# Spacing the groups of seven block products in a gated feed-forward loop: three plain units between groups instead of two

## The chip, the cores and the metric

The kernel runs on one core of a Trainium2 chip. The metric is the device time of one execution in microseconds (us). The engines that matter here are TensorE (PE in the profile; the loading of its stationary operand has a row of its own, PEld), VectorE (DVE), ScalarE (ACT) and SyncE (SP), which issues the transfers. Each engine runs its own instructions strictly in the order in which they are written; semaphores order them against one another.

## The reference

One block of a streaming encoder, for 256 tokens of width 2048:

```python
def swiglu(x, w_in, w_out):
    gate, up = jnp.split(x @ w_in, 2, axis=-1)
    return (jax.nn.silu(gate) * up) @ w_out

h = h + 0.5 * swiglu(rmsnorm(h, ffn1_norm[l]), ffn1_w_in[l], ffn1_w_out[l])
...   # gated mixing and stick-breaking attention, then cross attention
h = h + 0.5 * swiglu(rmsnorm(h, ffn2_norm[l]), ffn2_w_in[l], ffn2_w_out[l])
return rmsnorm(h, final_norm)
```

`w_in` is 2048 x 11264 (5632 gate columns, 5632 up columns). The change is in how `x @ w_in` is walked, in both feed-forward parts.

## The kernel before, in words

**Split products.** All data are 32-bit. Each operand is held as a high part (ACT copies the raw values, rounded, into `w_hi`) and a low part (DVE subtracts, `w_lo = raw - w_hi`), and each product is three matmuls: hi x hi, hi x lo, lo x hi. So every weight needs a transfer, one ACT instruction and one DVE instruction before TensorE may read it.

**Units and the ring.** A unit is 128 x 1024 weights (512 KB): two blocks of 128 rows by 512 columns. Units pass through a ring of four slots. SP may load unit p into its slot once the low part of unit p-4 is done (`load`, semaphore `w_lo_done`). ACT may write `w_hi` of unit p once TensorE is done with unit p-4 (`split`, semaphore `w_used`).

**A pair.** The hidden columns go in 11 chunks of 512. The first chunk is done plainly; the other ten are the loop `Fori(1, FJ)`, one gate chunk and one up chunk together, called a pair: 16 units, numbered 0 to 15. Ten pairs in each feed-forward part, 20 in all. A pair has three groups (`FAST = 3`, s = 0, 1, 2; called groups 1, 2 and 3 here) and ten plain units. A plain unit is 12 matmuls. A group takes two units, in which four weight blocks are laid out so that seven block products (21 matmuls) do the work of eight: it needs sums of weight blocks, which DVE makes (`weight_sums`, four additions of 128 x 512, into `raw` and `t_raw`), ACT rounds (`t_hi_part`) and DVE subtracts (`t_lo_part`). The first two of the seven products need only the units themselves; the other five wait for `t_lo_part`. The products of the groups go partly into banks of their own: `sum_p1` and `sum_p5` (tile `tp`), `sum_p6` and `sum_p7` (tile `aux`).

**The order of a pair on DVE.** For each group: the four sums (`L1314` to `L1323`), which first wait for both units of the group to have landed; `w_lo` of its two units (`L1190`); `t_lo_part` (`L1335`); then `w_lo` of the plain units after it. After group 1's first plain unit stands `up_drained` (`L1290`), and among group 2's sums stand the two halves of `hidden` (`L1297`), both for the pair before. After group 3 and `w_lo` of unit 12 come, in this order: the transpose of the hidden chunk of the pair before, fetched by SP (`turn`, `L1230`); `sum_p6` plus a copy of `sum_p1` (`L1352`), which waits for ACT's copy (`p1_copied`); the low part of the hidden chunk (`fill_lo`, `L1198`), which waits for ACT's high part (`L735`); `w_lo` of unit 13; three additions that finish the gate (`L1356`, `L1361`, `L1363`); `w_lo` of unit 14; one subtraction (`L1368`); `w_lo` of unit 15. Then the next pair begins.

**ACT** runs beside it: `w_hi` of the units (`L728`), `t_hi_part` (`L825`), and between the `w_hi` of units 12 and 13 a wait for TensorE to be done with group 3 (`w_used` up to `FAST_END`), the copy of `sum_p1` (`L837`) and the high part of the hidden chunk (`L735`); after unit 14 the silu (`L844`), and then unit 15.

**SP** issues the 16 loads of a pair in order, and between them `send` (the hidden chunk to a buffer in device memory, 512 KB, once `hid_done` says that it is there) and `fetch` (four transfers that bring it back in turned order, once `send` has landed).

Of the kernel before, what the change touches and what calls it, by code (L numbers as in the profile page):

```python
# [29 lines left out]


FAST = 3


def pair_order():

    plain = [(0, u) for u in range(FAST, U8)] + [(1, u) for u in range(FAST, U8)]
    order = []
    for s in range(FAST):
        order += [("fast", s), ("fast", s)] + plain[:2]  # L40
        plain = plain[2:]
    return order + plain


# [2 lines left out]

FAST_END = FAST_AT[-1] + 2

GATE_END = PAIR_ORDER.index((0, U8 - 1)) + 1  # L50
UP_START = PAIR_ORDER.index((1, FAST))

SEND_AT = 10
FETCH_AT = 12

X_MIX_AT = [5, 7, 9]
H3_MIX_AT = [9, 11, 13]
# [132 lines left out]
def encoder_block(nc, x, x_cols, mem, mem_cols, first_cols, ws_cols, ffn1_w_in, ffn1_w_out, w_mix_in,  # L190
# [8 lines left out]
    with ctx:  # L199
# [511 lines left out]
        def _(eng):  # L711
# [8 lines left out]
            def split(base, n, u, length=U8, after_long=False, wait=True):  # L720

                loads = slot_loads(base, u % RING) + u // RING + rate(u, length) * n

                eng.wait_ge(w_loaded[u % RING], 16 * loads + 16)
                if wait:

                    eng.wait_ge(w_used, base + length * n + (u - ring_distance(u, after_long) + 1))
                eng.activation(w_hi[:, u % RING], raw[:, u % RING], ACT.Copy).then_inc(w_hi_done, 1)  # L728
# [72 lines left out]
            def ffn_in(base, rs, first, hid, first_hi):  # L801

                def silu(gate_used):

                    eng.wait_ge(stat_out, stat(rs) + 1)

                    eng.wait_ge(w_used, gate_used)

                    eng.wait_ge(mix_lo_done, FAST * (fast_pairs[base] > 0) + FAST)
                    for t in range(NT):  # L810
                        last = eng.activation(stage[:, t], acc[:, t], ACT.Silu,
                                              scale=rstd[:, stat(rs), t:t + 1])
                    last.then_inc(silu_done, 1)

                def fast_hi(j, s):


                    p = FAST_AT[s]
                    eng.wait_ge(t1_done, fast_count(base, j, s) + 1)
                    split(base, j, p, PAIR)  # L820
                    split(base, j, p + 1, PAIR)
                    eng.wait_ge(t_summed, fast_count(base, j, s) + 1)
                    if s:
                        eng.wait_ge(t_used, fast_count(base, j, s))
                    eng.activation(t_hi_part[:], t_raw[:], ACT.Copy).then_inc(t_hi_done, 1)  # L825

                def pair(j, hid_dst):

                    for s in range(FAST):
                        fast_hi(j, s)  # L830
                        split(base, j, FAST_AT[s] + 2, PAIR)
                        split(base, j, FAST_AT[s] + 3, PAIR)
                    for p in range(4 * FAST, PAIR - 3):
                        split(base, j, p, PAIR)

                    eng.wait_ge(w_used, base + PAIR * j + FAST_END)
                    eng.activation(copy_p1, sum_p1, ACT.Copy).then_inc(p1_copied, 1)  # L837
                    fill_hi(turned, number(TURNS, hid) + j, hid_dst, src=stage4)
                    split(base, j, PAIR - 3, PAIR)
                    split(base, j, PAIR - 2, PAIR)  # L840

                    eng.wait_ge(gate_added, fast_pairs[base] + j)
                    for t in range(NT):
                        last = eng.activation(stage[:, t], stage[:, t], ACT.Silu,  # L844
                                              scale=rstd[:, stat(rs), t:t + 1])
                    last.then_inc(silu_done, 1)
                    split(base, j, PAIR - 1, PAIR)

                first(silu)
                with eng.Fori(1, DC + 1) as j:  # L850
                    pair(j, first_hi[:, bass.ds(4 * j - 4, 4), :])
                with eng.Fori(DC + 1, FJ) as j:
                    pair(j, hid_hi[:, bass.ds(4 * j - 4 - KT, 4), :])
# [323 lines left out]
        def _(eng):  # L1177
# [106 lines left out]
            def ffn_in(base, rs, first, hid, first_hi, first_lo):  # L1284
                def up_drained(j):


                    eng.wait_ge(gate_read, silus[base] + 1 + j)
                    eng.wait_ge(w_used, base + PAIR + PAIR * j)
                    eng.tensor_tensor(shared[:], acc[:, NT:2 * NT], shared[:], ALU.subtract).then_inc(up_read, 1)  # L1290
# [34 lines left out]
                def unit_lo(j, p):  # L1325

                    split(p, base + PAIR * j + p)
# [10 lines left out]
                def pair(j, hi, lo):  # L1338
                    done = fast_pairs[base] + j

                    for s in range(FAST):
                        fast_lo(j, s)
                        unit_lo(j, FAST_AT[s] + 2)
                        if s == 0:
                            up_drained(j - 1)
                        unit_lo(j, FAST_AT[s] + 3)
                    for p in range(4 * FAST, PAIR - 3):
                        unit_lo(j, p)
                    turn(number(TURNS, hid) - 1 + j, stage4)

                    eng.wait_ge(p1_copied, done)
                    eng.tensor_tensor(shared[:, 0], sum_p6, copy_p1, ALU.add).then_inc(p6_added, 1)  # L1352
                    fill_lo(split_number(hid) - 1 + j, lo, hi, src=stage4)
                    unit_lo(j, PAIR - 3)
                    eng.wait_ge(p6_added, done)
                    eng.tensor_tensor(shared[:, 1], shared[:, 0], sum_p7, ALU.subtract).then_inc(p7_added, 1)  # L1356

                    eng.wait_ge(w_used, base + PAIR * j + GATE_END)

                    eng.wait_ge(t_read, number(FILLS, hid) + j)  # L1360
                    eng.tensor_tensor(stage[:, 0], acc[:, 0], copy_p1, ALU.add)  # L1361
                    eng.wait_ge(p7_added, done)
                    eng.tensor_tensor(stage[:, 1], acc[:, 1], shared[:, 1], ALU.add).then_inc(gate_added, 1)  # L1363
                    unit_lo(j, PAIR - 2)

                    eng.wait_ge(gate_added, done)
                    p5 = sum_p5.rearrange("p (a n) -> p a n", a=1).broadcast_to([P, NT, CH])
                    eng.tensor_tensor(shared[:], shared[:], p5, ALU.subtract).then_inc(gate_read, 1)  # L1368
                    unit_lo(j, PAIR - 1)
# [495 lines left out]
        def _(eng):  # L1865
# [29 lines left out]
            def ffn_in(base, hi, lo, first):  # L1895
# [6 lines left out]
                def block_of(k, t):  # L1902
                    rows = slice(t * P, (t + 1) * P)
                    return hi[:, k, rows], lo[:, k, rows]
# [7 lines left out]
                def fast(j, s):  # L1912


                    p = FAST_AT[s]
                    unit = base + PAIR * j + p
                    start, stop = s == 0, s == FAST - 1
                    s3, s1, s2 = [(mix_hi[s][:, i], mix_lo[s][:, i]) for i in range(3)]
                    eng.wait_ge(w_lo_done, unit + 1)
                    three(sum_p1, block_of(UK * s, 0), ring_block(p, 1), start, stop)  # L1920
                    three(sum_p5, s1, ring_block(p, 0), start, stop).then_inc(w_used, 1)

                    eng.wait_ge(t_lo_done, fast_count(base, j, s) + 1)
                    three(sum_p7, s3, sum_block(0), start, stop)
                    three(sum_p6, s2, sum_block(1), start, stop)
                    three(acc[:, 1], block_of(UK * s + 1, 1), sum_block(2), start, False).then_inc(t_used, 1)

                    eng.wait_ge(w_lo_done, unit + 2)
                    three(acc[:, 0], block_of(UK * s + 1, 0), ring_block(p + 1, 0), start, False)
                    if s == 0:  # L1930
                        eng.wait_ge(up_read, silus[base] + j)
                    three(acc[:, NT], block_of(UK * s, 1), ring_block(p + 1, 1), start, False).then_inc(w_used, 1)

                def plain(j, p):

                    side, u = PAIR_ORDER[p]
                    eng.wait_ge(w_lo_done, base + PAIR * j + p + 1)
                    for i in range(UK):
                        for t in range(NT):
                            start = p == UP_START and i == 0 and t == 1  # L1940
                            stop = u == U8 - 1 and i == UK - 1
                            last = three(acc[:, NT * side + t], block_of(UK * u + i, t), ring_block(p, i), start, stop)
                    last.then_inc(w_used, 1)

# [417 lines left out]
```

## Time and profile before

| | |
|---|---|
| median of 3 runs | 2129.9 us (2128.22 to 2129.93) |
| the profiled execution | 2127.3 us, its span 2125.4 us |
| TensorE busy | 2107.7 us, 99% of the span |
| VectorE busy | 1530.6 us (72%); in the pair loops 355.1 us of 381.7 |
| ScalarE busy | 1093.8 us (51%) |
| DMA | 472.37 MB, 222 GB/s on average |
| granted TensorE clock | 1.00 in each of the stretches read |

The page's busy shares are for the whole span. The first part's pair loop lies from 49 to about 474 us, the second's from 1454 to about 1878 us; what is between and behind them has no groups and isn't touched. "Start to start" below means the distance between the start times of two rows of the trace, which is the pace at which an engine takes its instructions; the durations printed overlap a little at both ends.

### The profile page before, as it was taken

The page shows a single profiled execution, that of the slowest core. Times are in us where ns is not written, and L with a number is a line of the kernel's source. Part 1 is how long each engine was busy: PE and PEld are TensorE (multiplying, and loading weights), DVE is VectorE, ACT ScalarE, POOL GpSimd, SP SyncE. Part 2 cuts the span into 40 slices and gives each one's busy share as a digit, 9 for nine tenths or more (in the row PEclk, how much of TensorE's full clock was granted, in tenths as well). Part 3 has the DMA queues.
Part 4 walks back from the last instruction along what each step waited for, and adds up shares of the span by engine and source line. Part 5 has one row for each costly group of instructions (what it writes and reads, how often), then busy time and mean ns, then how long its engine had stood idle before and what let it go on. Part 6 is the DMA issues. An engine that isn't in the chain of part 4 may idle for free.

```text
span 2125.4 us, 27293 instructions
## 1 busy us (share of the span) xinstructions
PE 2107.7 (99%) x9405; PEld 1738.6 (82%) x9405; DVE 1530.6 (72%) x1647; ACT 1093.8 (51%) x1251; POOL 38.3 (2%) x50
## 2 busy tenths in 40 slices
PE   9999999999999999999999999999999999999998
PEld 7778888878888888888888888887888887888887
DVE  8989999984555576566565656569999999964444
ACT  7555555553444465456544545555555555543433
POOL 0000000000000030000000000000000000000000
PEclk9999999999999999999999999999999999999999
DMA  8676667676566676765487766576667666785554
GB/s 297 212 236 224 218 221 234 222 257 228 203 234 210 227 258 217 241 215 185 175 286 239 235 208 195 187 243 209 219 214 236 226 217 211 238 286 195 191 187 157
DMA packets 185317, 472.37 MB, mean 222 GB/s; under 512 B 17056, under 2 KB 67616, under 8 KB 185120
## 3 DMA queue, kind: packets, MB, share of 16 engines
q1 hardware_dynamic: 183088, 464.11, 65.3%
q0 software_dynamic: 1728, 6.82, 0.9%
q8 instruction: 42, 0.69, 0.1%
q10 hardware_dynamic: 432, 0.53, 0.1%
q14 instruction: 27, 0.22, 0.0%
HBM read 443.60 MB, written 27.79 MB: 222 GB/s over the span
## 4 chain that ended last, share of the span: by engine, by line
PE 60%; DVE 18%; issue 9%; DMA 9%; ACT 3%; DVEq 0%; ACTq 0%; SPq 0%; POOL 0%; POOLq 0%
PE acc L1875 18%; PE acc L1878 18%; PE acc L1877 18%; DMA raw<-in_ffn_w_in 9%; DVE w_lo L1190 8%; DVE t_raw L1319 2%; DVE raw L1315 2%; DVE t_raw L1314 2%; ACT w_hi L728 1%; DVE stage L1230 1%; PE acc L2035 1%; DVE t_raw L1323 1%; DVE stage L1297 1%; PE acc L1899 1%; PE acc L1898 1%
## 5 line engine op out<-in xcount | busy, mean ns | idle before, releaser
L1190 DVE TENSOR_TENSOR w_lo<-raw,w_hi 128x1024 fp32r<-128x1024 f32 x765 | 924.1, 1223 | 476.1 <-ACT w_hi L728 473.5
L728 ACT ACTIVATE w_hi<-raw 128x1024 fp32r<-128x1024 f32 x765 | 794.4, 1055 | 839.0 <-PE acc L1878 530.6
L1875 PE MATMUL acc<-w_hi,a_hi 128*128 128x512 f32 x744 | 290.0, 390 | 0.0
L1877 PE MATMUL acc<-w_lo,a_hi 128*128 128x512 f32 x744 | 289.6, 389 | 0.0
L1878 PE MATMUL acc<-w_hi,a_lo 128*128 128x512 f32 x744 | 289.5, 389 | 0.0
L1875 PE MATMUL acc<-w_hi,b_hi 128*128 128x512 f32 x576 | 225.6, 392 | 0.0
L1878 PE MATMUL acc<-w_hi,b_lo 128*128 128x512 f32 x576 | 224.2, 389 | 0.0
L1877 PE MATMUL acc<-w_lo,b_hi 128*128 128x512 f32 x576 | 224.2, 389 | 0.0
L1898 PE MATMUL acc<-w_hi,b_hi 128*128 128x512 f32 x460 | 179.0, 389 | 0.0
L1898 PE MATMUL acc<-w_hi,a_hi 128*128 128x512 f32 x460 | 179.0, 389 | 0.0
L1899 PE MATMUL acc<-w_lo,b_hi 128*128 128x512 f32 x460 | 178.9, 389 | 0.0
L1900 PE MATMUL acc<-w_hi,a_lo 128*128 128x512 f32 x460 | 178.9, 389 | 0.0
L1899 PE MATMUL acc<-w_lo,a_hi 128*128 128x512 f32 x460 | 178.9, 389 | 0.0
L1900 PE MATMUL acc<-w_hi,b_lo 128*128 128x512 f32 x460 | 178.9, 389 | 0.0
L1875 PE MATMUL acc<-w_hi,hid_hi 128*128 128x512 f32 x432 | 168.0, 389 | 0.0
L1877 PE MATMUL acc<-w_lo,hid_hi 128*128 128x512 f32 x432 | 168.0, 389 | 0.0
L1878 PE MATMUL acc<-w_hi,hid_lo 128*128 128x512 f32 x432 | 168.0, 389 | 0.0
L1875 PEld LDWEIGHTS acc<-w_hi,a_hi 128*128 128x128 f32 x744 | 139.7, 188 | 29.6 <-issue 0.9
L1878 PEld LDWEIGHTS acc<-w_hi,a_lo 128*128 128x128 f32 x744 | 139.7, 188 | 29.1
L1877 PEld LDWEIGHTS acc<-w_lo,a_hi 128*128 128x128 f32 x744 | 139.7, 188 | 28.7
L1878 PEld LDWEIGHTS acc<-w_hi,b_lo 128*128 128x128 f32 x576 | 108.1, 188 | 22.7
L1875 PEld LDWEIGHTS acc<-w_hi,b_hi 128*128 128x128 f32 x576 | 108.2, 188 | 22.4 <-issue 0.8
(276 smaller groups left out, 2645.0 us busy)
## 6 DMA issues: line engine op xcount, KB each, us to landing
raw<-in_ffn_w_in SPq DMA_DIRECT2D x349, 512.0 KB, 4.3
raw<-in_ffn_w_out SPq DMA_DIRECT2D x176, 512.0 KB, 4.3
raw<-in_w_mix_in SPq DMA_DIRECT2D x80, 512.0 KB, 4.4
raw<-in_w_ckv SPq DMA_DIRECT2D x64, 512.0 KB, 4.3
memq<-bounce SPq DMA_DIRECT2D x196, 128.0 KB, 3.4
bounce<-stage SPq DMA_DIRECT2D x37, 512.0 KB, 6.1
raw<-in_w_mix_out SPq DMA_DIRECT2D x32, 512.0 KB, 4.4
raw<-in_w_cq SPq DMA_DIRECT2D x32, 512.0 KB, 4.3
```

Source lines behind the costliest of these rows:

```text
L728: eng.activation(w_hi[:, u % RING], raw[:, u % RING], ACT.Copy).then_inc(w_hi_done, 1)
L1190: eng.tensor_tensor(w_lo[:, u % RING], raw[:, u % RING], w_hi[:, u % RING].bitcast(f32), ALU.subtract).then_inc(w_lo_done, 1)
L1230: eng.transpose(dst.rearrange("p k (b j) -> p b k j", j=32), xs.rearrange("p b (k i) -> p b k i", i=32)).then_inc(turned, 1)
L1314: eng.tensor_tensor(t_raw[:, 0], b12, b22, ALU.add)
L1315: eng.tensor_tensor(b12, b12, b11, ALU.add).then_inc(t1_done, 1)
L1319: eng.tensor_tensor(t_raw[:, 1], b12, b22, ALU.add).then_inc(t2_done, 1)
L1875: eng.matmul(dst, x_hi[:, rows], w_hi[:, slot, i], start=start and i == 0, stop=False)
L1877: eng.matmul(dst, x_hi[:, rows], w_lo[:, slot, i], start=False, stop=False)
L1878: last = eng.matmul(dst, x_lo[:, rows], w_hi[:, slot, i], start=False, stop=stop and i == UK - 1)
L1898: eng.matmul(dst, x[0], w[0], start=start, stop=False)
L1899: eng.matmul(dst, x[0], w[1], start=False, stop=False)
L1900: return eng.matmul(dst, x[1], w[0], start=False, stop=stop)
```

## The change

The order of a pair gets three plain units after group 1 and three after group 2 (`BETWEEN = 3`), where it had two, and so four after group 3 instead of six. The groups now take units 0 and 1, 5 and 6, 10 and 11 (before: 0 and 1, 4 and 5, 8 and 9). The ten plain units keep their order among themselves. `send` moves from ahead of load 10 to ahead of load 9, `fetch` from ahead of load 12 to ahead of load 13. The wait of the gate additions on TensorE (`GATE_END`) now names the end of group 3, since the gate's last plain unit comes before it. `FAST_END`, which ACT's copy of `sum_p1` waits for, is unit 12 instead of 10 in number: the end of group 3 in both. What each engine does after `w_lo` of unit 12 keeps its order.

```diff
+BETWEEN = 3
...
     for s in range(FAST):
-        order += [("fast", s), ("fast", s)] + plain[:2]
-        plain = plain[2:]
+        order += [("fast", s), ("fast", s)] + plain[:BETWEEN]
+        plain = plain[BETWEEN:]
     return order + plain
...
-GATE_END = PAIR_ORDER.index((0, U8 - 1)) + 1
+GATE_END = FAST_END
...
-SEND_AT = 10
-FETCH_AT = 12
+SEND_AT = 9
+FETCH_AT = 13
...  (ACT)
                     for s in range(FAST):
                         fast_hi(j, s)
-                        split(base, j, FAST_AT[s] + 2, PAIR)
-                        split(base, j, FAST_AT[s] + 3, PAIR)
-                    for p in range(4 * FAST, PAIR - 3):
-                        split(base, j, p, PAIR)
+                        for p in range(FAST_AT[s] + 2, (FAST_AT + [PAIR - 3])[s + 1]):
+                            split(base, j, p, PAIR)
...  (DVE)
                     for s in range(FAST):
                         fast_lo(j, s)
-                        unit_lo(j, FAST_AT[s] + 2)
-                        if s == 0:
-                            up_drained(j - 1)
-                        unit_lo(j, FAST_AT[s] + 3)
-                    for p in range(4 * FAST, PAIR - 3):
-                        unit_lo(j, p)
+                        for p in range(FAST_AT[s] + 2, (FAST_AT + [PAIR - 3])[s + 1]):
+                            unit_lo(j, p)
+                            if p == FAST_AT[0] + 2:
+                                up_drained(j - 1)
...  (PE, flags that end an accumulation)
-                    three(acc[:, 1], block_of(UK * s + 1, 1), sum_block(2), start, False).then_inc(t_used, 1)
+                    three(acc[:, 1], block_of(UK * s + 1, 1), sum_block(2), start, stop).then_inc(t_used, 1)
...
-                    three(acc[:, 0], block_of(UK * s + 1, 0), ring_block(p + 1, 0), start, False)
+                    three(acc[:, 0], block_of(UK * s + 1, 0), ring_block(p + 1, 0), start, stop)
...
-                            stop = u == U8 - 1 and i == UK - 1
+                            stop = side == 1 and u == U8 - 1 and i == UK - 1
```

**DVE, from group 3's `t_lo_part` to the hidden chunk's low part, in the first pair loop.** Before, three `w_lo` (units 10, 11, 12) stand between `t_lo_part` and the transpose:

```order
L1335 TENSOR_TENSOR t_lo_part<-t_raw,t_hi_part 128x1536
L1189 REGISTER_ALU
L1190 TENSOR_TENSOR w_lo<-raw,w_hi 128x1024
L1189 REGISTER_ALU
L1190 TENSOR_TENSOR w_lo<-raw,w_hi 128x1024
L1189 REGISTER_ALU
L1190 TENSOR_TENSOR w_lo<-raw,w_hi 128x1024
L1229 ISA
L1230 STREAM_TRANSPOSE stage<-memq 128x8x4x32
L1352 TENSOR_TENSOR shared<-aux,arrived 128x512
```

The same place in the changed kernel (its line numbers are one to three lower) has one, unit 12:

```order
L1334 TENSOR_TENSOR t_lo_part<-t_raw,t_hi_part 128x1536
L1188 REGISTER_ALU
L1189 TENSOR_TENSOR w_lo<-raw,w_hi 128x1024
L1228 ISA
L1229 STREAM_TRANSPOSE stage<-memq 128x8x4x32
L1349 TENSOR_TENSOR shared<-aux,arrived 128x512
```

Two `w_lo` have gone from this stretch, and nothing behind it has moved.

**DVE, from group 2's `t_lo_part` to group 3's sums, same loop.** Before there are two `w_lo` between (units 6 and 7):

```order
L1335 TENSOR_TENSOR t_lo_part<-t_raw,t_hi_part 128x1536
L1189 REGISTER_ALU
L1190 TENSOR_TENSOR w_lo<-raw,w_hi 128x1024
L1189 REGISTER_ALU
L1190 TENSOR_TENSOR w_lo<-raw,w_hi 128x1024
L1310 ISA
L1314 TENSOR_TENSOR t_raw<-raw 128x512
```

Now there are three (units 7, 8 and 9):

```order
L1334 TENSOR_TENSOR t_lo_part<-t_raw,t_hi_part 128x1536
L1188 REGISTER_ALU
L1189 TENSOR_TENSOR w_lo<-raw,w_hi 128x1024
L1188 REGISTER_ALU
L1189 TENSOR_TENSOR w_lo<-raw,w_hi 128x1024
L1188 REGISTER_ALU
L1189 TENSOR_TENSOR w_lo<-raw,w_hi 128x1024
L1309 ISA
L1313 TENSOR_TENSOR t_raw<-raw 128x512
```

The third stands ahead of the sums in the queue; the stretch after group 1 gets a third `w_lo` in the same way.

**SP, around `send`, same loop.** Before (the rows from load 8 on; `bounce<-stage` is `send`):

```order
L450 DMA raw<-in_ffn_w_in 128x1024
L450 ISA [waits w_lo_done]
L450 DMA raw<-in_ffn_w_in 128x1024
L457 ISA [waits hid_done]
L457 DMA bounce<-stage 128x2x512
L450 ISA [waits w_lo_done]
L450 DMA raw<-in_ffn_w_in 128x1024
```

After:

```order
L451 DMA raw<-in_ffn_w_in 128x1024
L458 ISA [waits hid_done]
L458 DMA bounce<-stage 128x2x512
L451 ISA [waits w_lo_done]
L451 DMA raw<-in_ffn_w_in 128x1024
L451 ISA [waits w_lo_done]
L451 DMA raw<-in_ffn_w_in 128x1024
```

`send` and its wait have moved ahead of load 9.

## Rows read from the trace of the kernel before

**Rows 1.** The page, section 1: busy time of each engine over the whole span
```profile
PE 2107.7 (99%) x9405; PEld 1738.6 (82%) x9405; DVE 1530.6 (72%) x1647; ACT 1093.8 (51%) x1251; POOL 38.3 (2%) x50
```

**Rows 2.** Who waited for whom, whole span: us in total, times, longest us
```profile
DVE t_raw L1314 <- issue: 37.2, 20, 2.9
...
ACT arrived L837 <- PE acc L1900: 29.6, 20, 1.9
...
PEld aux L1898 <- DVE t_lo_part L1335: 24.2, 40, 1.6
```

**Rows 3.** Stretches of nine pairs: us, PE, PEld, DVE, ACT, POOL busy, clock, DMA share, GB/s
```profile
49.44:431.18 381.74, 377.83 (x1648) 307.75 (x1647) 355.11 (x371) 208.57 (x209) 0.00 (x0) 1.00 0.68 223
1454.43:1836.47 382.04, 377.57 (x1649) 307.70 (x1647) 353.41 (x370) 207.78 (x207) 0.00 (x0) 1.00 0.68 222
```

**Rows 4.** TensorE in order of time, group 3 of pair 5 to pair 6
```profile
243.12 0.50 PE L1898 MATMUL aux<-t_hi_part,mix_hi 128*128 128x512 f32 x1 [0.26 <-DVE t_lo_part L1335]
...
246.42 0.39 PE L1900 MATMUL acc<-w_hi,a_lo 128*128 128x512 f32 x1
246.65 0.39 PE L1898 MATMUL acc<-w_hi,a_hi 128*128 128x512 f32 x1
...
262.97 0.39 PE L1898 MATMUL tp<-w_hi,a_hi 128*128 128x512 f32 x1
```

**Rows 5.** DVE in order of time, same stretch: start, us, what, [idle before]
```profile
236.38 0.69 DVE L1314 TENSOR_TENSOR t_raw<-raw 128x512 f32<-128x512 f32 x1 [1.80 <-issue]
...
242.98 3.49 DVE L1190 TENSOR_TENSOR w_lo<-raw,w_hi 128x1024 fp32r<-128x1024 f32 x3
246.39 1.23 DVE L1230 STREAM_TRANSPOSE stage<-memq 128x1024 f32<-128x1024 f32 x1
247.55 0.65 DVE L1352 TENSOR_TENSOR shared<-aux,arrived 128x512 f32<-128x512 f32 x1
248.99 1.23 DVE L1198 TENSOR_TENSOR hid_lo<-stage,hid_hi 128x1024 f32 x1 [0.79 <-ACT hid_hi L735]
250.14 1.22 DVE L1190 TENSOR_TENSOR w_lo<-raw,w_hi 128x1024 fp32r<-128x1024 f32 x1
...
253.07 1.22 DVE L1190 TENSOR_TENSOR w_lo<-raw,w_hi 128x1024 fp32r<-128x1024 f32 x1
...
255.51 1.23 DVE L1190 TENSOR_TENSOR w_lo<-raw,w_hi 128x1024 fp32r<-128x1024 f32 x1
256.65 0.68 DVE L1314 TENSOR_TENSOR t_raw<-raw 128x512 f32<-128x512 f32 x1
...
259.31 2.35 DVE L1190 TENSOR_TENSOR w_lo<-raw,w_hi 128x1024 fp32r<-128x1024 f32 x2
261.58 1.75 DVE L1335 TENSOR_TENSOR t_lo_part<-t_raw,t_hi_part 128x1536 fp32r<-128x1536 f32 x1
263.25 1.22 DVE L1190 TENSOR_TENSOR w_lo<-raw,w_hi 128x1024 fp32r<-128x1024 f32 x1
264.38 1.22 DVE L1290 TENSOR_TENSOR shared<-acc,shared 128x1024 f32<-128x1024 f32 x1
...
266.65 0.68 DVE L1314 TENSOR_TENSOR t_raw<-raw 128x512 f32<-128x512 f32 x1
...
270.38 2.35 DVE L1190 TENSOR_TENSOR w_lo<-raw,w_hi 128x1024 fp32r<-128x1024 f32 x2
```

**Rows 6.** ACT in order of time, same stretch
```profile
246.85 0.60 ACT L837 ACTIVATE arrived<-tp 128x512 f32<-128x512 f32 x1 [1.65 <-PE acc L1900]
247.76 1.06 ACT L735 ACTIVATE hid_hi<-stage 128x1024 f32 x1 [0.32 <-DVE stage L1230]
```

**Rows 7.** The chain that ended last, around pairs 5 and 6: start, us, what
```profile
230.81 3.77 DMA raw<-in_ffn_w_in
...
261.83 4.29 DMA raw<-in_ffn_w_in
```

**Rows 8.** SP's issues in order of time
```profile
231.34 0.41 SPq L457 DMA_DIRECT2D bounce<-stage  x1
```

## The prediction

> **What bounds the kernel now.** I read the page first: TensorE is busy for 2107.7 of 2125.4 us [rows 1], so at first sight nothing but its own pace counts. The waits show where the missing time is: the load of the first operand after `t_lo_part` waited 24.2 us in 40 of the 60 groups, DVE stood idle before a group's sums 37.2 us in 20 cases (one per pair, always group 3), and ACT waited 29.6 us, 20 times, for TensorE's end of group 3 before it copied `sum_p1` [rows 2]. Then I took the pair loops alone: nine pairs last 381.74 us in the first part and 382.04 in the second, so a pair takes 42.43 us. DVE is busy 39.4 us of each (355.11 and 353.41 over nine), at a granted clock of 1.00 [rows 3]. TensorE's own pace: from 246.65 to 262.97 it starts 72 matmuls (six plain units), 0.2267 us each [rows 4]. 183 matmuls make 41.5 us. So a pair loses only about 0.9 us to stalls, 17 us over 20 pairs, and that is the whole prize if every stall in the groups went.
>
> DVE is thus 3 us per pair from being the bound itself, and where its work stands matters more than how much there is. The reader should follow one pair on DVE and ask, for each group, when `t_lo_part` is done and when TensorE wants it. TensorE wants it six matmuls (1.36 us) after the group starts. Before group 1 of pair 6 DVE was done at 263.25 [rows 5], TensorE wanted it at 262.97 + 1.36 = 264.33 [rows 4]: a slack of 1.1 us after a stretch in which TensorE had 93 matmuls (21.1 us) to do.
>
> **The change part by part.** No instruction is added or removed on TensorE, ACT or DVE: the same 183 matmuls and the same 39.4 us of DVE work per pair, and the flags that end an accumulation change no duration, 0 us. What changes is how much work of each engine lies between the three deadlines. TensorE's stretches become 57, 57 and 69 matmuls (12.92, 12.92 and 15.64 us) instead of 45, 45 and 93 (10.20, 10.20, 21.08). I time everything from A, the start of the first matmul on `t_lo_part` in a group (243.12 for group 3 [rows 4]).
>
> *Group 3 to the next group 1.* Before, DVE did three `w_lo`, the transpose and then `sum_p6`, which needs ACT's copy. The last matmul of group 3 starts at 246.42 [rows 4], the copy at 246.85, which is A + 3.73, and it takes 0.60 [rows 6]: ready at A + 4.33. DVE began the `sum_p6` step at 247.55 = A + 4.43 [rows 5], just as its earlier work ran out. Now two `w_lo` of 1.13 us each (start to start, 263.25 to 264.38 [rows 5]) are gone from ahead of it. DVE has finished the transpose by A + 2.2, but the copy still comes at A + 4.33, because it hangs on TensorE's 15 matmuls and not on DVE. So the 2.27 us that DVE no longer does here turn into idle time, and the `sum_p6` step stays at A + 4.43. What does get earlier is ACT's high part of the hidden chunk: it started at 247.76 only because the transpose was late [rows 6], and would now follow the copy directly at A + 4.33. The low part starts 1.23 after it (247.76 to 248.99 [rows 5, 6]), at A + 5.56 instead of A + 5.87. From there to the end of the next group 1's `t_lo_part` (248.99 to 263.25 [rows 5]) lie 14.26 us of DVE work with hardly a gap: fill, units 13, 14, 15, the gate's additions, four sums, two `w_lo`, `t_lo_part`. Ready at A + 19.82, and with the 0.14 from there to the matmul (242.98 to 243.12 [rows 4, 5]) the next A is at **A + 19.96**. Before it was A + 21.21 (262.97 + 1.36 - 243.12), set by TensorE. TensorE now has only 15.64 + 0.14 us of work there: it stalls for 4.2 us, spread over units 13 and 14, the first products of group 1 and the five behind them, the longest about 1.6 us (unit 13's `w_lo` is ready at A + 7.84, and unit 12 ends at A + 6.3).
>
> *Group 1 to group 2.* DVE's order is unit 2, `up_drained`, unit 3, unit 4, the sums with `hidden`, two `w_lo`, `t_lo_part`. Its work is 3.40 (263.25 to 266.65) + 1.13 + 3.73 (266.65 to 270.38) + 2.27 (259.31 to 261.58) + 1.67 (261.58 to 263.25) = 12.20 us [rows 5]. Its sums wait for load 6, which may be issued once unit 2's `w_lo` is done, 1.13 in. Load 5 took 4.29 us there [rows 7]; with 0.1 to issue and 0.2 to start, the sums begin at 5.7 instead of 4.5. That gives 5.75 + 3.73 + 2.27 + 1.67 = **13.42**, against TensorE's 12.92 (13.06 with the 0.14 of a restart). If the load lands in 3.77, as the other one in those rows did, TensorE's 13.06 stands.
>
> *Group 2 to group 3.* Three `w_lo`, sums, two `w_lo`, `t_lo_part`: 3.40 + 6.60 (236.38 to 242.98 [rows 5]) = 10.0 us. The sums wait for load 11, issued after unit 7's `w_lo`: 1.13 + 0.1 + 4.3 + 0.2 + 6.60 = 12.3, below TensorE's **12.92**, which I take. The other bound: before, from the end of unit 5's `w_lo` at 230.65 (228.37 + 2.28) to the sums at 236.38 went 5.7 us, idle 1.80 at the end [rows 5, 7], while `send` was issued at 231.34 [rows 8], right behind load 9. If load 11 suffers as much, 1.13 + 5.7 + 6.60 = 13.4. I take the lower, because `send` now goes out during group 2's sums, some 5 us ahead of load 11. `send` needs only `hidden`, which is done by then, so load 9 behind it waits for nothing new, and `fetch` has until A + 1 of group 3, over 10 us: 0 us for both.
>
> The Trainium skill ("DMA: Bandwidth & Descriptors", Anatomy of one DMA) puts a transfer at about 2.0 us fixed plus its bytes over 436 GB/s. By that a 512 KB load would take 3.2 us, an estimate from that page, and group 1 to 2 would be 13.06 instead of 13.42: 6 us less in the sum. The trace's loads of 3.77 and 4.29 us [rows 7] don't agree, so the sum goes by them.
>
> *The sum.* A pair: 19.96 + 13.42 + 12.92 = 46.30 us, against 42.43: +3.87. Nine such distances in each part: 18 x 3.87 = 69.7. The tenth pair has no group 1 behind it. There the end is unit 15, whose `w_lo` starts at A + 12.08 (255.51 - 243.12 less the 0.31 gained [rows 5]), ends 1.14 later, and is followed by 0.14 and 12 matmuls: A + 16.08. With the other two stretches 42.4 us, against 177 x 0.2267 + 0.9 = 41.0 before: +1.4, twice 2.8. Together +72.5 us. The profiled execution's 2127.3 becomes 2199.8; the median of the runs shown lies 2.6 above it, so I say **2202 us**.
>
> **The rivals.**
>
> *The groups' stalls go, as the wider spacing between them would have it* (faster). Between groups 1 and 2, and 2 and 3, DVE gains 2.72 us of TensorE's time for 1.13 of work, so the waits of rows 2 would vanish there. If group 1 then weren't late either, a pair takes 41.5 us: 17 us less, about 2113. It decides at a DVE stretch after group 3 below 15.8 us. Against it: the work behind the copy alone is 14.26 + 1.23, on top of the 4.33 to the copy's end. 5%.
>
> *No measurable change*, if ACT and DVE found some 4 us of that stretch to fill elsewhere. Their orders are written out and strict: 4%. (Below 0.2%, 4 us, a measurement of this kernel can't be told from none.)
>
> *DVE's idle time is used* (slower, but less). If the copy weren't what `sum_p6` waits for, the stretch would be 263.25 - 242.98 = 20.27 less two `w_lo`, 18.0, and the pair 18.0 + 0.14 + 13.42 + 12.92 = 44.5: +37, about 2167. For it: DVE at 247.55 started when its own work ended, too, so those rows don't say alone which of the two it needed. Against it: the copy's end at 247.45. 9%.
>
> *Loads are late as well* (slower still): 5.7 us for both loads 6 and 11. Then 14.8 + 13.4 + 19.96 = 48.2: +104 with the tenth pairs, about 2234. 6%.
>
> *TensorE's clock falls.* It stalled for up to 1.6 us at a time before [rows 2] at a clock of 1.00 [rows 3]; now there are four stalls in one stretch. If a third of a pair's matmuls, 61, ran at the lower level (1.2 instead of 2.4 GHz), that is 61 x 0.2267 = 13.8 us more where DVE didn't hide it, and even half of it over 20 pairs gives +138 on top, about 2340. No single stall that I find is longer than those of before. 3%. The rule behind it, that TensorE drops to the lower clock after a stretch of idling, is the Trainium skill's ("TensorE: Matmul & The Clock Gate", What's actually happening); the trace, with its clock of 1.00 throughout, has no case of it.
>
> **How the numbers follow.** My forecast, slower by the copy and the serial work behind it, has 73%; its own range is 2188 (group 1 to 2 at 13.06, and 0.4 less after group 3 where ACT's steps overlap) to 2222 (one load at 5.7). The range leaves out the first two cases and the last three for the most part: **2182 to 2224**. Faster 5%, same 4%, slower 91%.
>
> **What would show it.** Right: a period of about 46 us; ACT's high part of the hidden chunk starting right at the copy's end; DVE idle some 2 us before the `sum_p6` step (`shared<-aux,arrived`), 20 times; TensorE waiting for `w_lo` in the last units and for `t_lo_part` in group 1, where it waited for nothing; DVE's idle time before group 3's sums nearly without effect. Wrong: TensorE still waiting mainly in groups 2 and 3, a stretch from group 3's A to group 1's well under 19 us, or a granted clock below 1.

## The result and the profile after

The changed kernel takes 2195.6 us (median of 4 runs, 2195.05 to 2197.13) against 2129.06 us before in the same comparison. The ratio is 1.0315, with a 95% interval of 1.0299 to 1.033: slower by 66.5 us. The profiled execution has a span of 2193.3 us, against 2125.4, 67.9 more.

The page's first section of the changed kernel answers to [rows 1]. TensorE's busy share went from 99% to 97%, although the span is 3.2% longer; DVE and ACT have the same work in a longer span:

```profile
PE 2123.6 (97%) x9405; PEld 1734.8 (79%) x9405; DVE 1534.3 (70%) x1647; ACT 1090.8 (50%) x1251; POOL 38.3 (2%) x50
```

Busy time between the starts of the first and the tenth pair, in both parts of the changed kernel, columns as in [rows 3]. The clock is 1.00, nine pairs last 411.91 and 413.53 us instead of 381.74 and 382.04, and the work of DVE in them is what it was (354.55 and 352.96, before 355.11 and 353.41):

```profile
49.67:461.58 411.91, 384.43 (x1648) 305.83 (x1647) 354.55 (x369) 205.55 (x207) 0.00 (x0) 1.00 0.65 206
1487.17:1900.70 413.53, 385.22 (x1649) 305.55 (x1647) 352.96 (x369) 204.73 (x206) 0.00 (x0) 1.00 0.65 204
```

The waits of the changed kernel (us in total, times, longest), beside [rows 2]. Its line numbers are one to three lower than before: L836 is the copy of `sum_p1`, L1349 the `sum_p6` step, L1189 `w_lo`, L1334 `t_lo_part`, L1313 the first of the sums:

```profile
ACT arrived L836 <- PE acc L1897: 101.5, 20, 5.7
DVE t_raw L1313 <- DMA raw<-in_ffn_w_in: 54.7, 28, 2.8
DVE shared L1349 <- ACT arrived L836: 50.4, 20, 3.2
...
PEld acc L1895 <- DVE w_lo L1189: 43.7, 40, 1.9
PEld aux L1895 <- DVE t_lo_part L1334: 37.5, 35, 1.6
...
PE acc L1895 <- DVE w_lo L1189: 29.0, 20, 1.5
PE aux L1895 <- DVE t_lo_part L1334: 22.9, 25, 1.2
```

Two waits are new. DVE waits for ACT's copy in every pair, 2.5 us each, and TensorE waits for `w_lo` in the last plain units. Neither had a row before.

One pair shows how they hang together. First TensorE in order of time, from group 3 to the next group 1 (A is 261.16 and then 280.87). It reaches group 3's `t_lo_part` products without a stall, then stalls three times, before unit 13, before the first products of group 1 and before the five behind them:

```profile
261.16 0.39 PE L1895 MATMUL aux<-t_hi_part,mix_hi 128*128 128x512 f32 x1
...
264.34 0.39 PE L1897 MATMUL acc<-w_hi,a_lo 128*128 128x512 f32 x1
...
268.89 0.50 PE L1895 MATMUL acc<-w_hi,a_hi 128*128 128x512 f32 x1 [1.45 <-DVE w_lo L1189]
...
278.06 0.50 PE L1895 MATMUL tp<-w_hi,a_hi 128*128 128x512 f32 x1 [0.51 <-DVE w_lo L1189]
...
280.87 0.50 PE L1895 MATMUL aux<-t_hi_part,mix_hi 128*128 128x512 f32 x1 [1.15 <-DVE t_lo_part L1334]
281.21 0.39 PE L1896 MATMUL aux<-t_lo_part,mix_hi 128*128 128x512 f32 x1
```

Then ACT in the same stretch: 5.20 us of waiting for group 3's last matmul, the copy, and at once the high part of the hidden chunk:

```profile
264.76 0.60 ACT L836 ACTIVATE arrived<-tp 128x512 f32<-128x512 f32 x1 [5.20 <-PE acc L1897]
265.25 1.05 ACT L736 ACTIVATE hid_hi<-stage 128x1024 f32 x1
```

And DVE: the transpose is over early, 2.59 us of idle time follow, and behind the copy the work runs on almost without a gap until `t_lo_part` of the next group 1 is done at 280.73:

```profile
253.82 0.69 DVE L1313 TENSOR_TENSOR t_raw<-raw 128x512 f32<-128x512 f32 x1 [2.22 <-DMA raw<-in_ffn_w_in]
...
260.42 1.22 DVE L1189 TENSOR_TENSOR w_lo<-raw,w_hi 128x1024 fp32r<-128x1024 f32 x1
261.56 1.24 DVE L1229 STREAM_TRANSPOSE stage<-memq 128x1024 f32<-128x1024 f32 x1
265.39 0.69 DVE L1349 TENSOR_TENSOR shared<-aux,arrived 128x512 f32<-128x512 f32 x1 [2.59 <-ACT arrived L836]
266.48 1.23 DVE L1197 TENSOR_TENSOR hid_lo<-stage,hid_hi 128x1024 f32 x1 [0.40 <-ACT hid_hi L736]
...
280.73 1.22 DVE L1189 TENSOR_TENSOR w_lo<-raw,w_hi 128x1024 fp32r<-128x1024 f32 x1
```

The first of these rows shows the other thing to see: DVE also waited 2.22 us for load 11 before group 3's sums, and it cost nothing, since TensorE came to group 3 later still.

**Three distances.** To compare kernels, I took from each timeline of TensorE the start A of the first matmul on `t_lo_part` in every group, and averaged the distances over the pairs of each part. The first number is the first feed-forward part, the second the other; "floor" is TensorE's own matmuls at 0.2267 us. This table is used for the experiments too.

| kernel | group 1 to 2 | 2 to 3 | 3 to the next 1 | a pair |
|---|---|---|---|---|
| before | 10.50, 10.35 | 10.75, 10.85 | 21.20, 21.23 | 42.35, 42.45 |
| its floor | 10.20 | 10.20 | 21.08 | 41.5 |
| changed | 13.17, 13.38 | 13.01, 13.05 | 19.71, 19.72 | 45.90, 46.11 |
| its floor | 12.92 | 12.92 | 15.64 | 41.5 |
| e2_spacing_alone | 13.41, 13.32 | 13.27, 13.62 | 19.79, 19.83 | 46.56, 46.70 |
| e3_chunk_first | 13.41, 13.42 | 13.05, 13.05 | 17.23, 17.19 | 43.73, 43.61 |
| e4_three_two | 13.50, 13.37 | 10.34, 10.31 | 19.70, 19.71 | 43.59, 43.37 |
| e5_four_two | 15.99, 15.94 | 10.39, 10.36 | 19.77, 19.75 | 46.15, 46.02 |
| e1_moved_transfers | 10.54, 10.33 | 10.85, 10.88 | 21.24, 21.23 | 42.63, 42.47 |
| e6_unit13_first | 10.33, 10.21 | 10.71, 10.46 | 21.24, 21.19 | 42.30, 41.78 |
| e8_send8 | 10.92, 10.82 | 10.34, 10.33 | 21.46, 21.32 | 42.70, 42.44 |
| e7_both | 10.40, 10.29 | 10.31, 10.32 | 21.08, 21.09 | 41.82, 41.72 |
| e10_send8_fetch13 | 10.29, 10.21 | 10.21, 10.23 | 21.08, 21.08 | 41.59, 41.53 |
| e9_both_fetch13 | 11.02, 10.71 | 10.35, 10.33 | 21.22, 21.16 | 42.57, 42.20 |

Measured from A to A, nine pairs are 31.9 and 32.9 us longer in the changed kernel, 64.9 together. (The stretches above gave 30.2 and 31.5: they end where the tenth pair starts, before the stalls of its group 1.) The remaining 3.0 of the 67.9 lie behind the A of the tenth pairs' group 1 and at the ends.

The text also gives, for single loads, the time from issue to landing, as the median over the pairs of one part. Load 9 is the load of unit 9 of a pair, and so on.

### The profile page after: what moved, and what is told of

The parts are those of the page before. It is cut to its first block, busy times and chain, and to the rows that moved or that the text cites. A ratio compares the mean times of both kernels' runs of the same rounds, so it can differ in the third digit from the quotient of the medians.

```text
span 2193.3 us, 27333 instructions
## 1 busy us (share of the span) xinstructions
PE 2123.6 (97%) x9405; PEld 1734.8 (79%) x9405; DVE 1534.3 (70%) x1647; ACT 1090.8 (50%) x1251; POOL 38.3 (2%) x50
## 4 chain that ended last, share of the span: by engine, by line
PE 77%; DVE 10%; issue 6%; DMA 3%; ACT 3%; DVEq 0%; ACTq 0%; SPq 0%; POOLq 0%; POOL 0%
PE acc L1872 18%; PE acc L1875 18%; PE acc L1874 18%; PE acc L1895 5%; PE acc L1897 5%; PE acc L1896 5%; DVE w_lo L1189 4%; DMA raw<-in_ffn_w_in 2%; DVE t_lo_part L1334 2%; PE aux L1895 1%; PE aux L1896 1%; PE aux L1897 1%; ACT w_hi L729 1%; DVE t_raw L1318 1%; DVE raw L1314 1%
## 5 line engine op out<-in xcount | busy, mean ns | idle before, releaser
L1189 DVE TENSOR_TENSOR w_lo<-raw,w_hi 128x1024 fp32r<-128x1024 f32 x765 | 923.8, 1224 | 464.9 <-ACT w_hi L729 462.4
L1895 PE MATMUL acc<-w_hi,a_hi 128*128 128x512 f32 x460 | 181.4, 394 | 14.5 <-DVE w_lo L1189 14.5
L1895 PE MATMUL acc<-w_hi,b_hi 128*128 128x512 f32 x460 | 181.4, 394 | 14.5 <-DVE w_lo L1189 14.5
```

What stands on the lines that cost most here:

```text
L1189: eng.tensor_tensor(w_lo[:, u % RING], raw[:, u % RING], w_hi[:, u % RING].bitcast(f32), ALU.subtract).then_inc(w_lo_done, 1)
L1895: eng.matmul(dst, x[0], w[0], start=start, stop=False)
```

## The experiments

Theory A, from the prediction: the loss is the serial work of ACT and DVE that starts when TensorE ends group 3, which four plain units no longer cover. The rivals on test: B, the moved transfers; C, DVE's whole work as the bound; D, the units between the groups and the loads that their sums wait for.

**The transfers moved alone, and the spacing alone.** First the kernel before with only the two constants of the change:

```diff
-SEND_AT = 10
-FETCH_AT = 12
+SEND_AT = 9
+FETCH_AT = 13
```

> The spacing of before (two and two), with send ahead of load 9 and fetch ahead of load 13. Theory A (the loss is the serial work that begins with ACT's copy at the end of group 3, which four plain units no longer cover): within 6 us of before, since the order of the units is that of before; a few us less if send then disturbs load 9 less. Rival B (the moved transfers make the group sums late): a good part of the 66 us, 2150 or more.

Measured: 2133.06 us against 2127.27, ratio 1.0027 (1.0017 to 1.0037). The 5.8 us are just within theory A's 6, with the sign that I had thought the less likely. Then the changed kernel with the constants put back to 10 and 12:

> The changed spacing, with send and fetch where before had them (ahead of loads 10 and 12). Theory A: 2190 to 2205, as the changed kernel or a few us above, since send then goes out just ahead of loads 10 and 11, on which group 3's sums wait. Rival B: back near 2130.

Measured: 2206.31 us, ratio 1.0367 (1.0344 to 1.039), 10.7 us above the changed kernel. So the spacing makes the whole loss, and in the changed kernel the moved transfers give some of it back. The table shows where: with `send` (issued at 250.02 in this timeline) just ahead of loads 10 and 11, group 2 to 3 goes from 13.01 and 13.05 to 13.27 and 13.62. The waits of this kernel say the same, 49 stalls on `t_lo_part` instead of 35:

```profile
PEld aux L1895 <- DVE t_lo_part L1334: 51.6, 49, 1.6
```

Rival B is out.

**The work that needs no copy put first.** The changed kernel, with this on ACT:

```diff
+                    split(base, j, PAIR - 3, PAIR)
+                    fill_hi(turned, number(TURNS, hid) + j, hid_dst, src=stage4)
                     eng.wait_ge(w_used, base + PAIR * j + FAST_END)
                     eng.activation(copy_p1, sum_p1, ACT.Copy).then_inc(p1_copied, 1)
-                    fill_hi(turned, number(TURNS, hid) + j, hid_dst, src=stage4)
-                    split(base, j, PAIR - 3, PAIR)
```

and on DVE:

```diff
+                    unit_lo(j, PAIR - 3)
+                    fill_lo(split_number(hid) - 1 + j, lo, hi, src=stage4)
                     eng.wait_ge(p1_copied, done)
                     eng.tensor_tensor(shared[:, 0], sum_p6, copy_p1, ALU.add).then_inc(p6_added, 1)
-                    fill_lo(split_number(hid) - 1 + j, lo, hi, src=stage4)
-                    unit_lo(j, PAIR - 3)
```

> The changed kernel, with the work that needs no copy of sum_p1 put ahead of the wait for it: on ACT the high parts of unit 13 and of the hidden chunk, on DVE w_lo of unit 13 and the low part of the chunk. Same instructions, other order. Theory A: the 2.6 us of idle time before the sum_p6 step and the 0.4 behind it are filled, the stretch from group 3 to group 1 falls from 19.7 to about 17.5 us, the pair from 45.9 to 43.7, the time by about 40 us to 2155. Rival C (a pair is long because DVE's whole work has become the bound, wherever its idle time stands): the idle time comes back elsewhere, 2190 or more.

Measured: 2150.87 us, ratio 1.0109 (1.0084 to 1.0134), 44.7 us less than the changed kernel. Group 3 to group 1 fell from 19.7 to 17.2 us; of the other distances only group 1 to 2 of the first part moved, up by 0.24. DVE in order of time shows the gap closed, `w_lo` of unit 13 and the chunk's low part standing where it idled:

```profile
254.85 1.24 DVE L1229 STREAM_TRANSPOSE stage<-memq 128x1024 f32<-128x1024 f32 x1
256.01 1.18 DVE L1189 TENSOR_TENSOR w_lo<-raw,w_hi 128x1024 fp32r<-128x1024 f32 x1
257.45 1.23 DVE L1197 TENSOR_TENSOR hid_lo<-stage,hid_hi 128x1024 f32 x1 [0.27 <-ACT hid_hi L736]
258.60 0.68 DVE L1351 TENSOR_TENSOR shared<-aux,arrived 128x512 f32<-128x512 f32 x1
```

The same instructions in another order give back two thirds of the loss, which rival C does not allow. The 17.2 us that are left are DVE's own work between the two groups: 20.27 before, less two `w_lo` (2.27) and the idle 0.79, is 17.2. TensorE has 15.6 of its own there.

**The same number of units behind group 3, otherwise spread.** The spacing as a list, `BETWEEN = [4, 2, 0]`, leaves four behind group 3 as the change does:

```diff
-BETWEEN = 3
+BETWEEN = [4, 2, 0]
...
-        order += [("fast", s), ("fast", s)] + plain[:BETWEEN]
-        plain = plain[BETWEEN:]
+        order += [("fast", s), ("fast", s)] + plain[:BETWEEN[s]]
+        plain = plain[BETWEEN[s]:]
```

> Four plain units after group 1, two after group 2, four after group 3 (the changed kernel: 3, 3, 4). Theory A: only the number behind group 3 counts, so the pair is 15.6 + 10.8 + 19.7 = 46.1 us and the time 2190 to 2205. Rival D (three units between groups are what costs, through the sums that wait for loads after each): another time than the changed kernel's by more than 15 us, since one of the stretches is now longer and one shorter.

Measured: 2198.46 us, ratio 1.0336 (1.0312 to 1.036), within 3 us of the changed kernel, and the distance behind group 3 is 19.75 again. With `[3, 2, 0]`, five behind group 3:

> Three plain units after group 1, two after group 2, five after group 3. Theory A: the stretch from group 3 to group 1 stays at the 19.7 us of its serial work, although TensorE now has 18.4 + 0.1 us of its own there; 13.2 + 10.8 + 19.7 = 43.7 us a pair, 1.3 above before, 2150 to 2157. Rival D (units between the groups cost, one by one): half of the 66 us, 2162.

Measured: 2145.76 us, ratio 1.0092 (1.0077 to 1.0108), below the range that I gave: group 2 to 3 took 10.3 and not 10.8, and group 1 to 2 13.4 to 13.5 and not 13.2. The waits on the copy, in this kernel and then in the other one, go with it (DVE waits about 0.7 us longer per pair with one unit fewer):

```profile
DVE shared L1349 <- ACT arrived L836: 31.0, 20, 1.9
```

```profile
DVE shared L1349 <- ACT arrived L836: 45.4, 20, 2.8
```

The distance from group 3 to group 1 is thus 19.7 us with four units behind group 3 and with five, whose floors are 15.6 and 18.4 us, and nearly TensorE's 21.1 with six. That is a constant length of serial work that six units cover and five don't.

Rival D, a cost per unit between the groups, is out by this run and the table. Five units between the groups instead of six should have left half of the 66 us, 2162. And the distances 1 to 2 and 2 to 3 lie only 0.1 to 0.7 us above TensorE's floor, with two, three or four units in between, the kernel before included. The run with four and two alone could not have told it: it has six units between the groups, as the change has.

**Toward a faster kernel.** In the kernel before, DVE idled twice in a pair: 1.80 us before group 3's sums, and 0.79 before the chunk's low part [rows 5]. First the second one. On DVE the low part and unit 13 change places, on ACT the `w_hi` of unit 13 goes ahead of the wait for group 3:

```diff
+                    split(base, j, PAIR - 3, PAIR)
                     eng.wait_ge(w_used, base + PAIR * j + FAST_END)
                     eng.activation(copy_p1, sum_p1, ACT.Copy).then_inc(p1_copied, 1)
                     fill_hi(turned, number(TURNS, hid) + j, hid_dst, src=stage4)
-                    split(base, j, PAIR - 3, PAIR)
...
                     eng.tensor_tensor(shared[:, 0], sum_p6, copy_p1, ALU.add).then_inc(p6_added, 1)
-                    fill_lo(split_number(hid) - 1 + j, lo, hi, src=stage4)
                     unit_lo(j, PAIR - 3)
+                    fill_lo(split_number(hid) - 1 + j, lo, hi, src=stage4)
```

> The kernel before with one change of order: w_lo of unit 13 ahead of the low part of the hidden chunk on DVE, its w_hi ahead of ACT's wait for group 3. It takes away the 0.79 us in which DVE waits for ACT behind the sum_p6 step. If DVE's chain of work sets the pace of the pairs before too, 0.4 to 0.8 us a pair: 2112 to 2120. If TensorE's own work and the loads of group 3 set it, no change, within 4 us of before.

Measured: 2122.39 us against 2126.52, ratio 0.9981 (0.9972 to 0.999). A gain of 4 us, short of the 2112 to 2120 of the one theory and at the edge of the other's 4 us. The idle time is gone from where it was and partly back before the `sum_p6` step, where the kernel before had no row:

```profile
DVE shared L1352 <- ACT arrived L838: 10.8, 15, 0.8
```

Then the first one, `send` ahead of load 8:

```diff
-SEND_AT = 10
+SEND_AT = 8
```

> The kernel before with send ahead of load 8 instead of load 10, so that it no longer runs right behind load 9, on which group 3's sums wait. If send is what delays load 9, DVE's idle time there (37 us in 20 pairs) falls by a third or more and the time by 5 to 12 us. If the load itself is what takes so long, within 4 us of before, or a little above as with send ahead of load 9.

Measured: 2132.65 us, ratio 1.0026 (1.0012 to 1.004): slower, although the wait that it was meant for did fall from 37.2 us to this:

```profile
DVE t_raw L1314 <- issue: 14.8, 20, 1.0
```

Load 9 now landed 4.4 us after its issue instead of 5.4, and group 2 to 3 is 0.4 to 0.5 us shorter. DVE in order of time shows where the gain is lost. `w_lo` of unit 12 waits for its `w_hi`, and in ACT's timeline that waited for load 12, which goes out behind `fetch` and landed 5.1 us after its issue instead of 3.8 (first part):

```profile
244.01 1.23 DVE L1190 TENSOR_TENSOR w_lo<-raw,w_hi 128x1024 fp32r<-128x1024 f32 x1 [0.81 <-ACT w_hi L728]
```

```profile
242.91 1.06 ACT L728 ACTIVATE w_hi<-raw 128x1024 fp32r<-128x1024 f32 x1 [1.43 <-DMA raw<-in_ffn_w_in]
```

DVE has no slack from here to group 2 of the next pair, so the 0.8 us come out there: from group 3 by way of group 1 to group 2 it takes 32.38 and 32.14 us, 0.68 and 0.56 more than before.

Both edits together:

> Both of the changes above in one: unit 13 first, and send ahead of load 8. If the gains are of one chain they add, down to where TensorE's 41.5 us a pair is the floor: at most 17 us under before, 2110 to 2118; else the better of the two alone.

Measured: 2115.44 us, ratio 0.9949 (0.9936 to 0.9963). That is 11 us below before, where the edits alone gave 4 less and 6 more. The range that I gave is met, but neither of its reasons: the two together are worth more than their sum and more than the better alone. The table fits the wait on load 12 being absorbed by the 0.79 us that the first edit frees: from group 3 to group 2 it takes 31.48 and 31.38 us, below the 31.70 and 31.58 of before. The next kernel moves `fetch` out of load 12's way, with `send` ahead of load 8 and the order of ACT and DVE as before:

```diff
-SEND_AT = 10
-FETCH_AT = 12
+SEND_AT = 8
+FETCH_AT = 13
```

> The kernel before with send ahead of load 8 and fetch ahead of load 13. With send alone moved, DVE's idle time before group 3's sums fell from 37 to 15 us, but a new wait of 0.8 us a pair stood before w_lo of unit 12, whose load goes out behind fetch, and the time rose. If load 12 behind fetch is what took the gain, it is gone here and the time is 2116 to 2124; if send running beside the loads of groups 2 and 3 costs by itself, it stays at 2127 or above.

Measured: 2111.98 us against 2127.37, ratio 0.9923 (0.991 to 0.9937), the fastest of all and better than expected. Load 12 lands 3.8 us after its issue again. A pair takes 41.59 and 41.53 us, TensorE's floor of 41.5. This kernel differs from the first experiment, the transfers moved alone, only in that `send` is ahead of load 8 and not of load 9, and takes 21 us less. Its page, and its busy time in nine pairs of the second part, in which TensorE has no idle time left:

```profile
PE 2099.2 (99%) x9405; PEld 1740.4 (82%) x9405; DVE 1534.6 (73%) x1647; ACT 1096.9 (52%) x1251; POOL 38.1 (2%) x50
```

```profile
1448.13:1821.88 373.75, 373.75 (x1649) 308.89 (x1647) 356.05 (x371) 209.19 (x207) 0.00 (x0) 1.00 0.70 228
```

Last, all three edits:

> Unit 13 first, send ahead of load 8 (together 2115 us) and fetch ahead of load 13. The pair was at 41.8 us, TensorE's own work is 41.5, so what is left to gain is 5 us: 2110 to 2116.

Measured: 2128.25 us, ratio 1.0007 (0.9998 to 1.0016). A clear miss. ACT in order of time shows why: with unit 13's `w_hi` ahead of the copy, the copy now also waits for load 13, and `fetch` stands ahead of exactly that load. DVE's row behind it is the idle time of the changed kernel once more:

```profile
248.89 1.06 ACT L728 ACTIVATE w_hi<-raw 128x1024 fp32r<-128x1024 f32 x1 [3.36 <-DMA raw<-in_ffn_w_in]
249.85 0.58 ACT L838 ACTIVATE arrived<-tp 128x512 f32<-128x512 f32 x1
```

```profile
250.47 0.69 DVE L1352 TENSOR_TENSOR shared<-aux,arrived 128x512 f32<-128x512 f32 x1 [2.48 <-ACT arrived L838]
```

## Why the prediction was right

It said 2202 us, 2182 to 2224; measured were 2195.6. Against the profiled executions the sum was +72.5 for a span that grew by 67.9; the rest of the difference is the 2.6 us that were added for the distance from the profiled execution to the median, which was 0.2 in the changed kernel. Term by term:

- *Group 3 to group 1:* said 19.96, measured 19.71 and 19.72. The mechanism is as predicted: the copy hangs on TensorE's 15 matmuls and not on DVE, so DVE's two `w_lo` less became 2.59 us of idle time, and ACT's high part followed the copy at once. In the pair shown TensorE stalled in three of the four places named; unit 14 had no stall. The 0.25 too much has two sources in the rows. Group 3 no longer started with a stall, so the copy came 3.60 after A (261.16 to 264.76) and not 3.73; and ACT starts its next instruction 0.49 behind the start of the copy, where I had counted its full 0.60.
- *Group 1 to 2:* said 13.42, measured 13.17 and 13.38. Load 6 landed 3.91 us after its issue in the first part and 4.31 in the second, where I took 4.29. In one pair of the first part unit 2's `w_lo` ended at 236.19 and the sums began at 240.15, 3.96 later instead of 4.6.
- *Group 2 to 3:* said 12.92, TensorE's floor, measured 13.01 and 13.05. Load 11 landed after 4.35 and 4.60 us, where I took 4.3. DVE's idle time there (2.22 in the pair shown) cost almost nothing, as said. The second spacing run shows that the choice of the lower bound hung on `send`: put next to loads 10 and 11, it would have been up to 13.62.
- *The pair:* said 46.30, measured 45.90 and 46.11. Eighteen distances gave 64.9 us where 69.7 were said.
- *The tenth pairs:* said 2.8, and 3.0 are left for them and the ends.
- *No cost for the moved `send` and `fetch`:* right for the change, though their place matters. In the changed kernel the move is worth 10.7 us (2195.6 with it, 2206.31 without), in the spacing of before it costs 6. The prediction had counted on the first in its choice of a bound, and not seen the second.
- *The clock:* the longest stall of the changed kernel was 1.9 us and the granted clock in the pair loops stayed at 1.00. By the Trainium skill ("TensorE: Matmul & The Clock Gate", What's actually happening) a stretch of idling brings the lower clock. No stall in a pair loop did that in any run here. The prediction was too quick to say that the trace has no case of it, since its end is one: the last matmul of the kernel before starts at 2118.34, and from 2123 to 2125 the granted clock is 0.50. TensorE has nothing left to do there, so it costs nothing.
- *A load's time:* By the Trainium skill ("DMA: Bandwidth & Descriptors", Anatomy of one DMA) a load of 512 KB would take an estimated 3.2 us. The Trainium skill gives that fit for transfers issued from GpSimd, and these are issued by SyncE. With 3.2 us the sum would have been 66, close to the 67.9, but by luck: load 6 took 3.9 and 4.3 us here, and the larger term that was too high lies behind group 3.

One reading of the rows was wrong. The 3.77 us in [rows 7] are not the time of a load. They are a piece of the chain that is cut off where DVE ran out of work, and the pieces behind it in the same view show it still waiting:

```profile
230.81 3.77 DMA raw<-in_ffn_w_in
234.58 1.80 issue
236.38 0.69 DVE t_raw L1314
```

That load, load 9, landed 5.5 us after its issue, which is the prediction's other bound, 5.7 us with the issue and the start. So the lower bound for group 1 to 2, 13.06, had no row under it; it held because load 6 does take less than 4.29 at times (4.08 in the median of the first part before, 3.91 after). Two sums are off without effect on the forecast. The prize of all stalls is 0.94 x 20 = 19 us, not 17. In the rival with both loads late, 5.7 us instead of 4.6 makes group 1 to 2 14.5 and not 14.8, and the rival +98 for the eighteen distances and not +104.

The rival that the idle time would be used, 2167 us, is settled by the trace and by the kernel with the chunk first: the copy does bind, and it took an edit of the order, to 2151 us, to use the time in front of it.

Open stays in part why `send` ahead of load 9 in the spacing of before costs 6 us. What the traces show is why it gains nothing. Load 9, on which group 3's sums wait, landed 5.6 and 5.5 us after its issue behind `send`, and 5.4 ahead of it; the wait before those sums is no smaller than before (38.7 us, 20 times). The two profiled executions differ by 4.3 us, of which 2.7 lie in the nine pairs of both parts and 1.8 ahead of the first pair's group 1. No run separates the rest.

## What to carry to other kernels

When an order is changed so that the same work stands elsewhere, sums over an engine say nothing: write down, for each deadline of the bound engine, which chain of the others starts after the last one, how long it is, and how much of the bound engine's own work covers it. A chain that begins with the bound engine's own result (here group 3, the copy, the gate, the next sums: 19.7 us) has a fixed length, and taking away work ahead of its first wait only makes idle time.

Filling an idle gap moves the work up to the next wait, and what that wait is for decides what is left of the gain. Here two fixes alone gave -4 and +6 us and together -11. Moving `fetch` by one load turned +6 into -15 in the one order of ACT and DVE, and -11 into +1 in the other, since there the copy stood behind the load that now goes out behind `fetch`. Follow a gain to the next deadline before counting it, and look which load every inserted transfer delays.

## What the runs showed of the hardware

- What is issued around a transfer of 512 KB changes its time by a factor. `send` landed 6.1 us after its issue (median) when it went out 0.5 us behind load 9 with load 10 to follow, and 2.8 us after it when it went out ahead of load 8, 3.1 us behind load 7. The median over all loads hardly changes, but single places do: load 9 went from 5.4 to 4.4 us, load 12 from 3.8 to 5.1, and the pieces of `fetch` from 3.2 to 5.1. What the transfers share is not shown here. The rows are of the transfers in the first pair loop, 60 to 428 us, of the kernel before and then of the one with `send` ahead of load 8:

```profile
raw<-in_ffn_w_in SPq DMA_DIRECT2D x140, 512.0 KB, 4.2
bounce<-stage SPq DMA_DIRECT2D x9, 512.0 KB, 6.1
memq<-bounce SPq DMA_DIRECT2D x36, 128.0 KB, 3.2
```

```profile
raw<-in_ffn_w_in SPq DMA_DIRECT2D x139, 512.0 KB, 4.3
memq<-bounce SPq DMA_DIRECT2D x36, 128.0 KB, 5.1
bounce<-stage SPq DMA_DIRECT2D x8, 512.0 KB, 2.8
```

- TensorE's first matmul after a stall takes 0.50 us in the rows and the next starts 0.34 behind it (280.87 to 281.21) instead of 0.23: each restart costs 0.11 us beside the wait.
